# Experts of a PEER layer in batches of one pair in place of two, with the turns between the dense steps spread twice as finely

## The chip, the cores and the metric

The kernel runs on one core of a Trainium2 chip. The metric is the device time of one execution in microseconds (us).

## The reference

The program is a decoder trunk of two layers for 256 tokens of width 1024, all in fp32. A layer is a mixer (attention in three forms, a convolution and a pooling branch), a cross-attention, and a block of single-neuron experts. The change touches the last of these:

```python
s_half = einsum('thpc,pnc->thpn', q, sub_keys)          # 8 heads, 2 halves, 128 keys
v_half, i_half = top_k(s_half, 16)
... top_s, expert_idx = top 16 of the 256 sums, per head
gate = softmax(top_s)
act = gelu(einsum('cd,chkd->chk', hc, u[ic]))           # u row of each chosen expert, times the token
out = einsum('chk,chkd->cd', gate * act, v[ic])         # v rows, weighted and summed
```

Each token chooses 8 x 16 = 128 experts of 16384. A chosen expert costs one row of u and one of v, 1024 numbers each, which lie side by side in memory.

## The kernel before

**Tiles and stages.** The tokens form two tiles of 128, one token to a partition. With two layers there are four pairs of layer and tile. The program has five stages, and a stage runs the dense part of one (layer, tile) beside the experts of the one before it: a first stage (dense alone), a second (dense, experts, and the keys and values of the memory for layer 1), two turns of a loop that share one code, and a last stage (experts alone, then the final norm). The dense part is written out as a plan of some sixty steps (`mix_norm`, `zq`, `ab`, ..., `wo0`, `wo1`, `xa_norm`, ..., `ffn_norm`, `pq0`, ..., `rank0`), in the order in which every engine takes its share of them.

**A pair.** One of the 128 (head, k) choices is called a pair here; it means one expert for each of the 128 tokens. For pair k:

- POOL (`gather`, L424) multiplies a stacked identity by the pair's gate into `diag` (L426), and issues an indirect DMA that brings 128 rows of u and v, 8 KB each, into one slot of `uv_rows` (L429). There are `ROWS` = 10 slots. For pairs from 10 on it waits for the semaphore `slots_free`, that is, for PE to be through with the pair that held the slot. At a stage's end the first ten pairs of the next are issued the same way.
- DVE (L461) takes the product of the u rows and the tokens in `h_ps`, with the sum into `act_b`.
- ACT (`batch_run`, below) takes the gelu and scales `diag` by it (L908).
- PE (L1154) adds `diag` times the v rows into `acc_pe`, in four matmuls, and signals `slots_free`.

**Batches and turns.** DVE, ACT and PE are in-order engines. Each has a function `batch_run(b0, b1)` that does its share of the batches b0 to b1, with B = 2 pairs to a batch. The function `run` walks through the plan; behind each step it does the number of batches that a table names. The function `spread` makes that table: each step has a weight in `LENGTH`, and the batches done by the end of a step are `within` times the share of weight passed, rounded down. PE's table is `LAG` batches behind that of DVE and ACT. What is left over at the end is done behind the last step. ACT's share of the batches reads:

```python
for b in range(b0, b1):
    act.wait_ge(sems["dots_done"], b * B + B)
    s.activation(gelu_b[:, b % AHEAD, :], act_b[:, b % AHEAD, :], ACT.Gelu_apprx_tanh).then_inc(sems["gelu_done"], 1)
    act.wait_ge(sems["gelu_done"], b + 1)
    for k in range(b * B, b * B + B):
        ...
        s.activation(diag[:, slot_of(k), :], diag[:, slot_of(k), :], ACT.Copy,
                     scale=gelu_b[:, b % AHEAD, k % B:k % B + 1]).then_inc(sems["diag_done"], 1)
```

PE waits for `diag_done` of each pair, and DVE for the landing of each pair. Gelu, exp and sqrt need different tables in ACT, and a load stands where the function changes; Copy needs none of its own.

**Other transfers.** The weights of the dense products come as blocks of 2 MB into a ring of two (`w_ring`); SP issues the next one when PE has finished with the one before last. They share the 16 DMA engines with the pairs.

Of the kernel before, what the change touches and what calls it, by code (L numbers as in the profile page):

```python
# [37 lines left out]
THETA, ROT = 500000.0, HD // 4  # L38
HALF = ROT // 2

B = 2
NB = PAIRS // B
QUARTER = NB // 4
AHEAD = 5
ROWS = AHEAD * B
HT = P // 2
BLK = 512
# [19 lines left out]
for _name, _w in (("causal", S), ("cadd", NC), ("cvalid", NC), ("cur", 4 * P), ("prev", 4 * P), ("flag", 1)):  # L67
# [64 lines left out]
LAST_PLAN = ["rank1", "rank_pairs1", "gates1", "look_up1", "rank2", "rank_pairs2", "gates2", "look_up2", "rank3",  # L132
             "rank_pairs3", "gates3", "look_up3"]
# [5 lines left out]
          "sel_turn": 4, "win_scores": 7, "sel_out": 8, "conv_norm": 4, "win_turn": 4, "conv_act": 3, "conv_silu": 2,  # L139
          "win_out": 8, "small_branches": 3, "mix_turn": 2, "wo": 9, "xa_norm": 7, "xq": 8, "xa_scores": 6,  # L140
          "xa_turn": 4, "xa_out": 4, "xo": 9, "ffn_norm": 8, "pq": 8, "sub_scores": 2, "mem_kv": 8}
LAG = 1


def spread(plan, within):

    lengths = [LENGTH[name if name in LENGTH else name.rstrip("0123456789")] for name in plan]
    vector, tensor, done, passed = {}, {}, 0, 0
    for name, length in zip(plan, lengths):
        passed += length  # L150
        due = within * passed // sum(lengths)
        vector[name] = due - done
        tensor[name] = max(due - LAG, 0) - max(done - LAG, 0)
        done = due
    return {"vector": vector, "scalar": vector, "tensor": tensor}


TURNS = spread(PLAN, NB - 2)
MEM_TURNS = spread(MEM_PLAN, NB - 2)
LAST_TURNS = spread(LAST_PLAN, 20)  # L160


TURN_PARTS = [6.25]
# [26 lines left out]
def build_program(nc, a):  # L190
    with ExitStack() as ctx:
        def sb(name, shape, dt=F32):
            return ctx.enter_context(nc.sbuf_tensor(name, shape, dt))
# [46 lines left out]
        gate = sb("gate", [P, PAIRS])  # L240
        act_b = sb("act_b", [P, AHEAD, B])
        gelu_b = sb("gelu_b", [P, AHEAD, B])
        half_i = sb("half_i", [P, 16, TOPK], U32)
# [44 lines left out]
        def stage(dense, experts, mem_layer=None, first=False, last=False):  # L288


            plan = LAST_PLAN if last else FIRST_PLAN if first else PLAN if mem_layer is None else MEM_PLAN
            turns = {} if first else LAST_TURNS if last else TURNS if mem_layer is None else MEM_TURNS
            jobs = [job for name in plan for job in STEP_JOBS.get(name, ())]
# [19 lines left out]
            def slot_of(k):  # L313
                return k % ROWS

            def landed_by(k):

                uses = len(range(k % ROWS, PAIRS, ROWS))
                return (experts * uses + k // ROWS) * 16 + 16
# [50 lines left out]
            with nc.Block(no_gpsimd_drain=not last) as block:  # L370
# [82 lines left out]
                def _(dve):  # L453
# [3 lines left out]
                    def batch_run(b0, b1):  # L457
                        for k in range(b0 * B, b1 * B):
                            dve.wait_ge(landed[slot_of(k)], landed_by(k))
                            u_row = uv_rows[:, slot_of(k), 0, :]  # L460
                            v.tensor_tensor_reduce(u_row, u_row, h_ps[:, :], 1.0, 0.0, ALU.mult, ALU.add,  # L461
                                                   act_b[:, k // B % AHEAD, k % B:k % B + 1]).then_inc(
                                                       sems["dots_done"], 1)
# [431 lines left out]
                def _(act):  # L895
# [3 lines left out]
                    def batch_run(b0, b1):  # L899
                        for b in range(b0, b1):  # L900
                            act.wait_ge(sems["dots_done"], b * B + B)
                            s.activation(gelu_b[:, b % AHEAD, :], act_b[:, b % AHEAD, :],  # L902
                                         ACT.Gelu_apprx_tanh).then_inc(sems["gelu_done"], 1)
                            act.wait_ge(sems["gelu_done"], b + 1)
                            for k in range(b * B, b * B + B):
                                if k >= ROWS:
                                    act.wait_ge(sems["gates_spread"], k - ROWS + 1)
                                s.activation(diag[:, slot_of(k), :], diag[:, slot_of(k), :], ACT.Copy,  # L908
                                             scale=gelu_b[:, b % AHEAD, k % B:k % B + 1]).then_inc(
                                                 sems["diag_done"], 1)  # L910
# [672 lines left out]
```

## Time and profile before

| | |
|---|---|
| median of 3 runs | 1901.41 us (1895.86, 1901.41, 1905.76) |
| the profiled execution, its own time | 1897.98 us |
| its span | 1896.2 us |
| what lies around the span | 1.8 us |
| TensorE clock granted, mean | 0.852 of full |
| PE, DVE, ACT, POOL busy | 1375.9, 1133.7, 514.9, 677.6 us |
| DMA | 702.57 MB, mean 371 GB/s |

The busy times are sums over stages with different limits, so none of them says what bounds the kernel. The share of the DMA engines is read by stretch of time, and where it falls below 1 the timeline shows which engine held the next transfer back. A window row gives the stretch and its length, the busy time of PE, of PE's weight loads, of DVE, ACT and POOL (with the count of instructions in brackets), then the granted clock, the DMA share and GB/s.

### The profile page before, as it was taken

The page shows a single profiled execution, that of the slowest core. Times are in us where ns is not written, and L with a number is a line of the kernel's source. Part 1 is how long each engine was busy: PE and PEld are TensorE (multiplying, and loading weights), DVE is VectorE, ACT ScalarE, POOL GpSimd, SP SyncE. Part 2 cuts the span into 40 slices and gives each one's busy share as a digit, 9 for nine tenths or more (in the row PEclk, how much of TensorE's full clock was granted, in tenths as well). Part 3 has the DMA queues.
Part 4 walks back from the last instruction along what each step waited for, and adds up shares of the span by engine and source line. Part 5 has one row for each costly group of instructions (what it writes and reads, how often), then busy time and mean ns, then how long its engine had stood idle before and what let it go on. Part 6 is the DMA issues. An engine that isn't in the chain of part 4 may idle for free. (4 is left out here: it accounts for less than half of the span.)

```text
span 1896.2 us, 23075 instructions
## 1 busy us (share of the span) xinstructions
PE 1375.9 (73%) x8428; PEld 714.3 (38%) x8428; DVE 1133.7 (60%) x2788; ACT 514.9 (27%) x1311; POOL 677.6 (36%) x1028
## 2 busy tenths in 40 slices
PE   6899956767889983946878863957878874555554
PEld 4666752234554551412444631422444631111110
DVE  5431359876342477689743567688743579864444
ACT  3331122154221222223522222223522221211111
POOL 0000025433333352534433351434433354555551
PEclk9899978889899996977989895977989887777776
DMA  7434589998999999999999998999999999999996
GB/s 272 178 151 178 199 355 399 423 422 353 364 364 399 371 422 409 371 422 403 421 415 397 395 420 346 379 422 400 421 413 397 390 421 371 404 423 421 421 421 268
DMA packets 87380, 702.57 MB, mean 371 GB/s; under 512 B 9952, under 2 KB 10080, under 8 KB 12128
## 3 DMA queue, kind: packets, MB, share of 16 engines
q0 software_dynamic: 73728, 536.90, 68.9%
q1 hardware_dynamic: 13536, 164.15, 21.9%
q8 instruction: 69, 1.13, 0.2%
q14 instruction: 47, 0.39, 0.1%
HBM read 698.92 MB, written 2.10 MB: 370 GB/s over the span
## 5 line engine op out<-in xcount | busy, mean ns | idle before, releaser
L1154 PE MATMUL acc_pe<-uv_rows,diag 64*64 64x512 f32 x4096 | 622.1, 741 | 346.4 <-ACT diag L908 338.0
L461 DVE CUSTOM_DVE_ANT_0 uv_rows<-uv_rows,h_ps 128x1024 f32<-128x1024 f32 x512 | 603.0, 1218 | 196.4 <-DMA uv_rows<-uv_in,idx 191.5
L426 POOL TENSOR_TENSOR diag<-ident_st,gate 128x64 f32<-128x64 f32 x512 | 167.4, 327 | 1097.5 <-PE acc_pe L1154 832.9
L429 POOL DMA_INDIRECT uv_rows<-uv_in,idx x512 | 510.1, 996 | 84.3 <-issue 51.2
L1154 PEld LDWEIGHTS acc_pe<-uv_rows,diag 64*64 64x64 f32 x4096 | 160.3, 158 | 726.6 <-ACT diag L908 501.1
L902 ACT ACTIVATE gelu_b<-act_b 128x2 f32<-128x2 f32 x256 | 51.9, 203 | 901.5 <-DVE act_b L461 891.1
L1181 PE MATMUL bank<-h_t,w_ring 128*128 128x128 f32 x1792 | 210.5, 279 | 11.3 <-DMA w_ring<-blocks_in 9.1
L1181 PEld LDWEIGHTS bank<-h_t,w_ring 128*128 128x128 f32 x1792 | 205.8, 195 | 31.8 <-issue 29.0
L1181 PE MATMUL bank<-w_ring,h_t 128*128 128x512 f32 x448 | 201.0, 603 | 3.0 <-ACTq L944 3.0
L908 ACT ACTIVATE diag<-diag,gelu_b 128x64 f32<-128x64 f32 x512 | 150.2, 340 | 8.4
L1181 PEld LDWEIGHTS bank<-w_ring,h_t 128*128 128x128 f32 x448 | 84.2, 193 | 119.5 <-issue 115.6
L748 DVE TENSOR_TENSOR xs<-xs,bank 128x512 f32<-128x512 f32 (+1 forms) x16 | 11.0, 688 | 179.0 <-PE bank L1181 179.0
L1176 PE MATMUL bank<-ident,area 128*128 128x128 f32 x304 | 51.3, 324 | 87.1 <-ACT area L921 67.3
L941 ACT ACTIVATE area<-bank 128x512 f32<-128x512 f32 x96 | 56.2, 586 | 207.5 <-PE bank L1181 195.8
L1176 PEld LDWEIGHTS bank<-ident,area 128*128 128x128 f32 x304 | 41.5, 167 | 112.8 <-ACT area L921 69.6
L585 DVE SCALAR_TENSOR_TENSOR conv<-hc,smalls,conv 128x128 f32<-128x128 f32 x240 | 67.4, 355 | 0.1
L902 ACT ACT_TABLE_LOAD x45 | 57.7, 1283 | 1.6
L760 DVE TENSOR_REDUCE st<-bank 128x2 f32<-128x512 f32 x8 | 5.5, 692 | 68.5 <-PE bank L1181 68.5
L461 DVE DVE_READ_ACCUMULATOR2_ANT act_b<- 128x1 f32 x512 | 42.3, 83 | 0.0
L1432 PE MATMUL acc_pe<-xs,zero 128*128 128x512 f32 x16 | 14.9, 1085 | 30.3 <-issue 17.1
L782 DVE MAX8 half_v<-area 128x8 f32<-128x128 f32 x64 | 13.9, 279 | 38.1 <-ACTq L944 38.0
L1016 ACT ACTIVATE area<-area,st 128x256 f32<-128x256 f32 x64 | 31.9, 499 | 12.4 <-DVE st L654 11.1
(200 smaller groups left out, 1173.9 us busy)
## 6 DMA issues: line engine op xcount, KB each, us to landing
w_ring<-blocks_in SPq DMA_DIRECT2D x72, 2048.0 KB
uv_rows<-uv_in,idx POOLq DMA_INDIRECT x512
tcon<-tile_consts_in SPq DMA_DIRECT2D x4, 656.5 KB, 13.0
smalls<-smalls_in SPq DMA_DIRECT2D x3, 816.5 KB, 8.5
h_ffn<-ffn_gain_in SPq DMA_DIRECT2D x4, 512.0 KB
xs<-x_in SPq DMA_DIRECT2D x2, 512.0 KB, 10.6
uv_rows<-mem_in SPq DMA_DIRECT2D x1, 1024.0 KB, 16.3
mem_gained<-uv_rows SPq DMA_DIRECT2D x1, 1024.0 KB, 4.8
```

The lines of the kernel that those rows point to most:

```text
L426: nc.gpsimd.tensor_tensor(diag[:, slot_of(k), :], ident_st[:, :], gate[:, k:k + 1].to_broadcast([P, HT]), ALU.mult).then_inc(sems["gates_s ...
L429: nc.gpsimd.indirect_dma_start(uv_rows[:, slot_of(k), :, :].rearrange("p a n -> p (a n)"), None, a["uv"], bass.IndirectOffsetOnAxis(ap=idx ...
L461: v.tensor_tensor_reduce(u_row, u_row, h_ps[:, :], 1.0, 0.0, ALU.mult, ALU.add, act_b[:, k // B % AHEAD, k % B:k % B + 1]).then_inc(sems[" ...
L585: ins = v.scalar_tensor_tensor(out=conv[:, g, :], in0=hc[:, g, k:k + P], scalar=small("cw", g * CONV_W + k, 1), in1=conv[:, g, :], op0=ALU ...
L902: s.activation(gelu_b[:, b % AHEAD, :], act_b[:, b % AHEAD, :], ACT.Gelu_apprx_tanh).then_inc(sems["gelu_done"], 1)
L908: s.activation(diag[:, slot_of(k), :], diag[:, slot_of(k), :], ACT.Copy, scale=gelu_b[:, b % AHEAD, k % B:k % B + 1]).then_inc(sems["diag_ ...
L941: drain(s.activation(out, src, func, **kw), job)
L1016: s.activation(probs[:, h, :], probs[:, h, :], ACT.Exp, bias=st[:, 8 + h:9 + h], accum_out=st[:, col + h:col + h + 1]).then_inc(sems[done], 1)
L1154: mm = pe.matmul(acc_pe[c * HT:(c + 1) * HT, r * BLK:(r + 1) * BLK], diag[tok, slot_of(k), :], uv_rows[tok, slot_of(k), 1, c * BLK:(c + 1) ...
L1176: mm = pe.transpose(out[:, i * P:(i + 1) * P], src, ident[:, :])
L1181: mm = pe.matmul(out, lhs, rhs, start=(i == 0), stop=(i == len(pairs) - 1))
L1432: pe.matmul(acc_pe[:, c * 512:(c + 1) * 512], zero[:, :], xs[:, 0:512], start=True, stop=False, skip_group_check=True)
```

## The change

Three tables and constants change, and no function body:

```diff
-B = 2
+B = 1
 NB = PAIRS // B
 QUARTER = NB // 4
-AHEAD = 5
+AHEAD = 10
 ROWS = AHEAD * B
...
-LAG = 1
+LAG = 2
...
-TURNS = spread(PLAN, NB - 2)
-MEM_TURNS = spread(MEM_PLAN, NB - 2)
-LAST_TURNS = spread(LAST_PLAN, 20)
+TURNS = spread(PLAN, NB - 4)
+MEM_TURNS = spread(MEM_PLAN, NB - 4)
+LAST_TURNS = spread(LAST_PLAN, 40)
```

A batch is one pair, so ACT takes a gelu of one column for each pair, 128 for each stage with experts in place of 64. The slots stay 10, the lag of PE stays two pairs, and the pairs left over at the end stay four. The tables of turns are rounded down to one pair in place of two: behind a step, as many pairs are done as before or one more. 

On PE, at the start of the loop's stage, stand the products with `zero` that clear `acc_pe`, the pairs (four matmuls each), the transposes of `mix_norm` into `bank`, and the products of `zq` (`bank<-w_ring,h_t`) and `ab` (`bank<-h_t,w_ring`). Before:

```order
L1432 MATMUL acc_pe<-xs,zero 128x512 x2
L1154 MATMUL acc_pe<-uv_rows,diag 64x512 x24
L1176 MATMUL bank<-ident,area 128x128 x8
L1154 MATMUL acc_pe<-uv_rows,diag 64x512 x8
L1181 MATMUL bank<-w_ring,h_t 128x512 x8
L1154 MATMUL acc_pe<-uv_rows,diag 64x512 x16
```

and now:

```order
L1432 MATMUL acc_pe<-xs,zero 128x512 x2
L1154 MATMUL acc_pe<-uv_rows,diag 64x512 x28
L1176 MATMUL bank<-ident,area 128x128 x8
L1154 MATMUL acc_pe<-uv_rows,diag 64x512 x8
L1181 MATMUL bank<-w_ring,h_t 128x512 x8
L1154 MATMUL acc_pe<-uv_rows,diag 64x512 x12
```

Seven pairs in place of six stand ahead of the transposes, nine in place of eight ahead of `zq`, and twelve in both ahead of `ab`.

On ACT, at the start of the second stage, stand the square sum of the norm (L917), its root (L919) and the scaling (L921), and the pairs. Before:

```order
L894 UNCONDITIONAL_BRANCH
L917 ACTIVATE h_t,st<-xs 128x1024
L919 ACT_TABLE_LOAD
L919 ACTIVATE st<-st 128x1
L921 ACTIVATE area<-xs,st 128x1024
L902 ACT_TABLE_LOAD
L902 ACTIVATE gelu_b<-act_b 128x2
L908 ACTIVATE diag<-diag,gelu_b 128x64 x2
```

and now:

```order
L894 UNCONDITIONAL_BRANCH
L902 ACT_TABLE_LOAD
L902 ACTIVATE gelu_b<-act_b 128x1
L908 ACTIVATE diag<-diag,gelu_b 128x64
L917 ACTIVATE h_t,st<-xs 128x1024
L919 ACT_TABLE_LOAD
L919 ACTIVATE st<-st 128x1
L921 ACTIVATE area<-xs,st 128x1024
```

The first pair, which waits for DVE's `rank1` and its own dot product, stands ahead of the norm.

On ACT, in the loop's stage, the exp of the compressed scores (L1021) is followed by the eight exps of the selected scores (L1016). Before:

```order
L1021 ACT_TABLE_LOAD
L1021 ACTIVATE p_cmp<-p_cmp 128x128
L1016 ACTIVATE area,st<-area,st 128x256 x8
L902 ACT_TABLE_LOAD
L902 ACTIVATE gelu_b<-act_b 128x2
L908 ACTIVATE diag<-diag,gelu_b 128x64 x2
```

and now:

```order
L1021 ACT_TABLE_LOAD
L1021 ACTIVATE p_cmp<-p_cmp 128x128
L902 ACT_TABLE_LOAD
L902 ACTIVATE gelu_b<-act_b 128x1
L908 ACTIVATE diag<-diag,gelu_b 128x64
L1016 ACT_TABLE_LOAD
L1016 ACTIVATE area,st<-area,st 128x256 x8
L902 ACT_TABLE_LOAD
```

One pair now parts the two groups of exps, with a table load ahead of it and one behind it. Over the program ACT gets 7 more table loads: 3 in the second stage and 2 in each turn of the loop.

## Rows read from the trace of the kernel before

**Rows 1.** The page: GB/s in 40 slices of the span.

```profile
GB/s 272 178 151 178 199 355 399 423 422 353 364 364 399 371 422 409 371 422 403 421 415 397 395 420 346 379 422 400 421 413 397 390 421 371 404 423 421 421 421 268
```

**Rows 2.** Windows: the second stage, the loop's two turns, the last stage.

```profile
258.00:714.00 456.00, 359.54 (x2183) 194.31 (x2184) 277.43 (x684) 130.52 (x328) 169.91 (x257) 0.89 0.97 393
714.00:1139.00 425.00, 302.17 (x1991) 154.31 (x1991) 278.66 (x684) 125.67 (x320) 170.96 (x256) 0.86 0.99 406
1139.00:1561.00 422.00, 310.87 (x1992) 157.89 (x1992) 279.11 (x685) 126.08 (x321) 170.16 (x256) 0.84 0.97 399
1561.00:1896.00 335.00, 183.36 (x1028) 44.90 (x1028) 209.42 (x465) 62.62 (x208) 153.65 (x236) 0.72 0.95 391
```

**Rows 3.** Timeline, DVE, last stage: two dot products, 20 pairs apart (start, length, ..., idle before).

```profile
1728.76 1.22 DVE L461 CUSTOM_DVE_ANT_0 uv_rows<-uv_rows,h_ps 128x1024 f32<-128x1024 f32 x1 [1.25 <-DMA uv_rows<-uv_in,idx]
...
1778.48 1.22 DVE L461 CUSTOM_DVE_ANT_0 uv_rows<-uv_rows,h_ps 128x1024 f32<-128x1024 f32 x1 [1.26 <-DMA uv_rows<-uv_in,idx]
```

**Rows 4.** Windows of single holes in the DMA share.

```profile
450.00:468.00 18.00, 14.41 (x97) 8.38 (x90) 6.36 (x14) 5.24 (x14) 7.90 (x12) 0.93 0.71 250
...
754.00:770.00 16.00, 14.88 (x64) 6.38 (x68) 14.26 (x32) 4.60 (x14) 3.82 (x6) 0.82 0.68 240
...
1174.00:1196.00 22.00, 15.69 (x68) 6.69 (x72) 15.99 (x40) 8.95 (x21) 3.91 (x7) 0.71 0.48 168
...
1574.00:1590.00 16.00, 7.70 (x52) 2.26 (x48) 13.16 (x29) 5.17 (x12) 9.91 (x14) 0.71 0.88 315
```

**Rows 5.** Timeline, the loop's second turn, around its `mix_norm`.

```profile
1172.27 1.22 DVE L461 CUSTOM_DVE_ANT_0 uv_rows<-uv_rows,h_ps 128x1024 f32<-128x1024 f32 x1
...
1173.42 1.22 DVE L461 CUSTOM_DVE_ANT_0 uv_rows<-uv_rows,h_ps 128x1024 f32<-128x1024 f32 x1
...
1182.28 3.69 PE L1154 MATMUL acc_pe<-uv_rows,diag 64*64 64x512 f32 x16 [0.83 <-DVE h_t L493]
...
1184.37 0.29 POOL L426 TENSOR_TENSOR diag<-ident_st,gate 128x64 f32<-128x64 f32 x1 [14.57 <-PE acc_pe L1154]
```

**Rows 6.** Timeline, the start of the last stage.

```profile
1567.37 1.22 DVE L461 CUSTOM_DVE_ANT_0 uv_rows<-uv_rows,h_ps 128x1024 f32<-128x1024 f32 x1
...
1574.21 0.29 POOL L426 TENSOR_TENSOR diag<-ident_st,gate 128x64 f32<-128x64 f32 x1 [0.29 <-PE acc_pe L1154]
...
1580.07 0.29 POOL L426 TENSOR_TENSOR diag<-ident_st,gate 128x64 f32<-128x64 f32 x1 [4.44 <-PE acc_pe L1154]
```

**Rows 7.** Timeline, the end of the last pair.

```profile
1878.71 1.22 DVE L461 CUSTOM_DVE_ANT_0 uv_rows<-uv_rows,h_ps 128x1024 f32<-128x1024 f32 x1 [1.22 <-DMA uv_rows<-uv_in,idx]
...
1880.61 3.69 PE L1154 MATMUL acc_pe<-uv_rows,diag 64*64 64x512 f32 x16 [3.22 <-ACT diag L908]
```

**Rows 8.** Timeline, the start of the second stage.

```profile
264.87 0.15 DVE L485 TENSOR_SCALAR st<-st 128x1 f32<-128x1 f32 x1
...
274.98 9.11 PE L1181 MATMUL bank<-h_t,w_ring 128*128 128x128 f32 x64 [6.31 <-DMA w_ring<-blocks_in]
...
285.22 0.29 POOL L426 TENSOR_TENSOR diag<-ident_st,gate 128x64 f32<-128x64 f32 x1 [27.01 <-PE acc_pe L1154]
```

**Rows 9.** Timeline, the loop's first turn, between `cmp_scores` and `sel_turn`.

```profile
886.37 0.51 ACT L1016 ACTIVATE area<-area,st 128x256 f32<-128x256 f32 x1
...
893.37 3.43 PE L1154 MATMUL acc_pe<-uv_rows,diag 64*64 64x512 f32 x16 [5.94 <-ACT diag L908]
...
902.48 0.20 DVE L660 RECIPROCAL st<-st 128x8 f32<-128x8 f32 x1
```

**Rows 10.** Timeline, PE ahead of the second stage's `wo0`.

```profile
463.91 1.95 PE L1154 MATMUL acc_pe<-uv_rows,diag 64*64 64x512 f32 x16 [2.01 <-ACT diag L908]
```

**Rows 11.** The page's groups: the gelu, the scaled `diag`, the table loads.

```profile
L902 ACT ACTIVATE gelu_b<-act_b 128x2 f32<-128x2 f32 x256 | 51.9, 203 | 901.5 <-DVE act_b L461 891.1
...
L908 ACT ACTIVATE diag<-diag,gelu_b 128x64 f32<-128x64 f32 x512 | 150.2, 340 | 8.4
L902 ACT ACT_TABLE_LOAD x45 | 57.7, 1283 | 1.6
```

## Prediction

> **What bounds the kernel now.** I began with the slices of GB/s [rows 1]. The first five slices move 151 to 272 GB/s, and from the sixth on the rate sits near 421 wherever it is not interrupted. No engine comes near its span. So from the second stage on the transfers are the limit, with holes. The windows by stage [rows 2] give the holes: against 422 GB/s, the second stage (456 us at 393) lacks 31 us of transfer, the loop's turns (425 at 406, 422 at 399) lack 16 and 23, and the last stage (335 at 391) lacks 25, of which 20 are the end, behind the last landing. In steady state a pair lands every (1778.48 - 1728.76) / 20 = 2.49 us [rows 3], which is the price of one pair in transfer time.
>
> A hole opens when all ten slots are waited for: ten pairs give 24.9 us of cover. I looked at who ends the wait. The largest hole, 1174 to 1196 [rows 4], lies in the loop's second turn: 22 us at 168 GB/s are 13.2 us without transfer. Its rows [rows 5] show DVE's dot products of a batch at 1172.27 and 1173.42; the norm follows on ACT, and PE takes that batch only behind the norm's transposes, at 1182.28. POOL had waited 14.57 us. The same place in the first turn (754 to 770) is a hole of 6.9 us, the one at 450 to 468 is 7.3 us, and the last stage has one of 4.1 us at 1574 to 1590 [rows 4]. So what the change is worth is read from when slots come free beside the dense steps.
>
> **The change, part by part.**
>
> *The gelu for each pair.* A first pair of a batch no longer waits for its neighbour's dot product. Two dots start 1173.42 - 1172.27 = 1.15 us apart [rows 5] (1.14 below), so the first of two slots comes free 1.14 us sooner where PE waits for it; the second comes when it did. The price is 256 more gelus of 203 ns [rows 11], 52 us of ACT over the 1638 us of rows 2, in which ACT is busy 445 us. For one pair ACT needs 0.20 + 0.34 and a gap, some 0.6 us, against 1.14 of DVE, so this is hidden under DVE; without that cover it would be 0.2 us a pair.
>
> *The table of turns.* Behind a step, 0 or 1 more pair is done. One more pair released ahead of a hole puts 2.49 us of transfer into it; its dot delays the dense chain behind it by 1.14 us, less the 0.25 by which the last diag of a batch is sooner. At the hole of rows 5, seven pairs stand ahead of the transposes in place of six, and nine in place of eight ahead of `zq`: gain 2.5 - 0.9 = 1.6 us. The end of the stage before adds something: PE's last two pairs were one batch, now only one is left behind the last dot, 0.98 us at the upper clock (1.95 for two [rows 10]). Sum 2.6 us for each turn, **5.2 us** for both. Behind this hole come stretches where DVE waits for transfers, so it is not given back.
>
> *Later holes of the loop.* Those at `wo0` and `ffn_norm` are small (the rest of the 16 and 23 us, in pieces of 1 to 4). PE is the chain there and by `pq0` one pair more has been done ahead of the norm, at a delay of about 0.9 us. I take 1 us for each turn, **2 us**; the bounds are 0 (the chain alone counts) and 2.49.
>
> *The second stage.* At its start the first pair moves ahead of the norm on ACT [rows 8]. The square sum lay under DVE's `rank1`, whose end shows as DVE's norm step at 264.87. Now it waits for `rank1` and a dot (1.22), the gelu and diag (0.6) and its own length (about 1.2): the norm step comes at 267.9 in place of 264.87, and then the root's table load (1.28), which lay under `rank1`, stands open. The norm is 4.4 us later. PE does not mind: `ab` waited 6.31 us for its weights until 274.98. The first slot now comes free at about 275 and not at 285.22, and that closes the 1.2 us hole of 282 to 286. DVE, which paces this stretch, loses 3.2 us and is one pair (1.14) ahead. I count +2 -1.2, about +1. Ahead of `wo0` PE waited 2.01 us for a fresh batch [rows 10]; only one fresh pair is needed now and the second need not be awaited: -2. Two norms (`xa_norm`, `ffn_norm`) are later by 1.05 and 0.8, and one pair more is done when the last hole of the stretch ends: -2.5. Sum about **-1.6 us**; bounds +4.4 (the whole delay of the norm on the chain, nothing won) and -7.
>
> *The last stage.* At its start the first slot needs one dot, not two, and three pairs in place of two are done ahead of `rank_pairs1`. The two gathers at 1574.21 and before are followed by none until 1580.07 [rows 6]; the third falls into this hole of 4.1 us: **-2.5 us**. What else the last stage lacks of its 25 us (25 - 20 - 4.1, about 1) I take as filled: **-1**; the bound is 0. At the end the last pair lands and its dot starts at 1878.71; PE then runs two pairs in 3.69 us [rows 7]; one remains: **-1.8 us**.
>
> *The table loads.* There are 7 more of 1283 ns [rows 11], 9.0 us on ACT. Those in the loop part the exps: the first exp at 886.37 [rows 9] moves by 1.28 + 0.54 + 1.28 = 3.1 us. PE then waits longer than its 5.94 us at 893.37, but DVE is busy without a pause through this stretch and needs the exps next at 902.48 [rows 9]; so I price the loads at nothing, with DVE as cover. Without the cover they cost 9.0, and the upper bound takes them.
>
> ScalarE: Activation LUTs in the Trainium skill ("What ACT_TABLE_LOAD costs") puts a switch at about 2.66 us, a load of 1283 ns and as much again for draining. The load's figure is the trace's own. With the drain the seven loads would come to 18.6 us; nothing in the rows here shows the drain as a time of its own.
>
> *Sum.* 5.2 + 2 + 1.6 + 2.5 + 1 + 1.8 = 14.1 us. Against the profiled execution (span 1896.2 plus 1.8 around it, 1897.98) this is 1884; that execution lies 3.4 us below the median of the runs shown, so on the scale of the median 1901.4 - 14.1 = **1887**.
>
> **Rivals.**
>
> - *Nothing but the end (no change).* The holes come back elsewhere: within a stretch where PE or DVE is the chain, one pair moved ahead leaves one fewer in the next turn (12 in both programs ahead of `ab`), and the hole behind is larger by what the one before lost. For it: in the second stage from 450 to 655 the holes come one after another. Against it: DVE waits for landings again behind both `mix_norm` holes and through the whole last stage, which keeps what was won. It leaves the tail and the start of the last stage, 1.8 + 2.5 = 4.3 of gain, and gives some of it back to the norm delays: 1898.
> - *ACT's share becomes the chain (slower).* Each norm that has one more pair ahead of it is later by about 1 us (2 in the second stage, 2 in each turn), the second stage's first norm by 4.4, and the parted exps push each turn by 3.1: 6 + 4.4 + 6.2 = 16.6, and only the tail (1.8) is won: 1916. It decides if slots wait for ACT in the stretch of rows 9, which takes a delay that eats up the time between PE's pairs at 893.37 and DVE's need at 902.48, 9 us. Against it: in that stretch the rate is at 421, with a backlog of several pairs.
> - *The clock.* In the last stage PE gets two pairs every 4.97 us, at a mean granted clock of 0.72 [rows 2]; it moves between 1.2 and 2.4 GHz. Now it gets one every 2.49. If the clock stayed at 1.2 GHz, a pair would take 1.85 us (3.69 for two), still under 2.49. The last stage would not feel it; a lower clock in the second stage's long products would, and 1% more PE time of 360 us is 3.6 us: 1891.
>
> **How the numbers follow.** The forecast (transfer holes partly filled, 1876 to 1892) gets 0.55; no change but the end, 0.28; slower through ACT, 0.12; the clock, 0.05. A measurement of this kernel can tell 0.5%, 9.5 us, from no change. Under 1892 lies most of the first case: faster 0.54. Slower than 1911 is most of the ACT case: 0.11. The rest, 0.35, is within. The range takes in the filling of every hole of one pair's size once (about 12 of 2.49 us, 30 us: 1872) and, on the other side, table loads uncovered (9.0) with nothing won but the tail, 1908. So 1872 to 1908.
>
> **What would show it.** Right: POOL's wait at the loop's `mix_norm` stays but one more gather lies ahead of it; GB/s in the slices with 346, 371 and 353 rises; the last PE group behind the last dot is 1.8 us long; the time of DVE at L461 is unchanged. Wrong: PE's waits for `diag` grow in sum outside the last stage; the second stage is longer than 456 us; `ab` starts later than 17 us into the second stage; the hole at 1174 is as long as before. If the second stage's start costs more than 3 us, or DVE turns out to wait for the parted exps, the prediction is too low.

## The result and the profile after

The changed kernel takes **1887.5 us** (median of 5 runs, 1883.99 to 1889.42) against 1900.24 us for the kernel before on the same chip (5 runs): a ratio of **0.9934**, 95% interval [0.9913, 0.9956]. That is 12.7 us less; the forecast was 14.1 less. The profiled execution took 1888.95 us (span 1887.2), 9.0 us less than that of before.

The page of the changed kernel: busy time of the engines, GB/s in 40 slices, and the groups that answer to [rows 11] (with PE's products for the pairs, which waited 338.0 us for `diag` before).

```profile
PE 1425.4 (76%) x8428; PEld 715.2 (38%) x8428; DVE 1133.2 (60%) x2788; ACT 595.8 (32%) x1574; POOL 675.3 (36%) x1028
...
GB/s 268 179 156 179 188 349 391 416 422 333 357 381 380 387 420 419 366 423 389 421 422 405 396 421 420 326 422 393 422 422 414 404 420 419 393 421 421 421 421 289
...
L1154 PE MATMUL acc_pe<-uv_rows,diag 64*64 64x512 f32 x4096 | 655.4, 754 | 306.1 <-ACT diag L908 293.2
...
L908 ACT ACTIVATE diag<-diag,gelu_b 128x64 f32<-128x64 f32 x512 | 178.1, 348 | 17.0 <-ACT gelu_b L902 0.2
...
L902 ACT ACTIVATE gelu_b<-act_b 128x1 f32<-128x1 f32 x512 | 102.5, 200 | 808.9 <-DVE act_b L461 788.1
L902 ACT ACT_TABLE_LOAD x49 | 62.9, 1283 | 9.2 <-issue 7.8
```

ACT does what was announced: 512 gelus of 200 ns, and over all its lines 111 table loads in place of 104. Nobody's total tells why the time fell; that is read by stage. The windows of the changed kernel for the stages of [rows 2], each from its own start:

```profile
259.00:718.50 459.50, 369.21 (x2184) 196.21 (x2184) 277.70 (x684) 151.37 (x395) 167.28 (x256) 0.86 0.96 390
718.50:1141.00 422.50, 315.31 (x1991) 158.19 (x1991) 278.17 (x684) 145.80 (x386) 171.48 (x256) 0.83 0.99 407
1141.00:1556.00 415.00, 315.34 (x1991) 158.43 (x1991) 278.74 (x684) 145.76 (x386) 171.25 (x256) 0.83 0.98 404
1556.00:1887.00 331.00, 205.59 (x1028) 39.39 (x1028) 209.43 (x465) 82.84 (x272) 152.11 (x236) 0.68 0.96 398
```

The second stage became longer, all the others shorter. The start of a stage is DVE's copy into `h_ps` in the timeline. Its lengths in us, for the kernels that the argument needs (one profiled execution each; the first stage, which has no pairs, differs by up to 3 us from one to the other, and so does this much of any sum). A profiled execution need not be a typical one: that of `e1` took 1884.83 us, its median is 1878.75. The loop is the same code in the changed kernel, `e3` and `e4`, and one of its turns differs by up to 5.8 us among them, so a smaller difference of one turn says little. The second stage repeats better (`e4`, `e8` and `e12` share it: 452.1, 452.1 and 453.1):

| | second | loop 1 | loop 2 | last |
|---|---|---|---|---|
| before | 455.8 | 425.2 | 421.5 | 335.4 |
| after | 459.6 | 422.7 | 415.0 | 331.1 |
| e1_old_tables | 455.0 | 419.8 | 415.2 | 331.7 |
| e2_old_tables_wait_two | 459.6 | 428.2 | 423.9 | 335.5 |
| e3_second_stage_old_table | 454.0 | 418.3 | 417.9 | 331.5 |
| e4_norm_first | 452.1 | 420.4 | 412.1 | 332.0 |
| e11_nine_slots | 466.7 | 427.6 | 426.4 | 333.5 |

Where the transfers stood still in a stretch is its length times (422 - GB/s) / 422, as in the prediction. Windows of the kernel before: the first 60 us of each turn of the loop (`mix_norm`), 100 us late in each turn (`wo0` to `ffn_norm`), and the first 100 us of the last stage.

```profile
714.00:774.00 60.00, 31.62 (x151) 12.97 (x152) 50.10 (x158) 14.71 (x36) 16.16 (x24) 0.70 0.92 372
...
974.00:1074.00 100.00, 84.21 (x549) 52.64 (x550) 41.72 (x96) 26.39 (x64) 33.19 (x52) 0.90 0.97 393
1139.00:1199.00 60.00, 32.26 (x143) 12.53 (x144) 50.12 (x158) 14.54 (x35) 15.39 (x23) 0.63 0.82 328
...
1399.00:1499.00 100.00, 82.56 (x534) 50.97 (x535) 40.15 (x87) 28.03 (x66) 34.15 (x53) 0.90 0.97 389
1561.00:1661.00 100.00, 53.49 (x292) 14.64 (x292) 90.26 (x269) 23.45 (x65) 48.03 (x71) 0.70 0.98 390
```

The same stretches of the changed kernel:

```profile
719.00:779.00 60.00, 33.14 (x147) 12.31 (x146) 50.53 (x160) 17.94 (x48) 16.36 (x24) 0.65 0.93 378
...
979.00:1079.00 100.00, 86.87 (x563) 53.74 (x564) 43.55 (x99) 29.87 (x78) 34.47 (x54) 0.88 0.99 401
1141.00:1201.00 60.00, 34.20 (x139) 12.18 (x140) 50.62 (x159) 17.64 (x46) 15.52 (x23) 0.64 0.86 345
...
1401.00:1501.00 100.00, 88.12 (x574) 55.56 (x575) 44.71 (x100) 29.43 (x78) 34.47 (x54) 0.87 1.00 408
1556.00:1656.00 100.00, 54.05 (x292) 14.18 (x292) 90.80 (x270) 29.36 (x83) 47.75 (x72) 0.70 1.00 406
```

Idle transfer time at `mix_norm` fell from 7.1 to 6.3 and from 13.4 to 10.9 us, late in the turns from 6.9 to 5.0 and from 7.8 to 3.3, at the start of the last stage from 7.6 to 3.8. So the late holes gave more than the large one. `e3` and `e4`, with the same loop, show how far such sums scatter: 15.2 and 14.3 us for both turns at `mix_norm` (20.5 before, 17.2 in the changed kernel), 4.3 and 2.6 late (14.7 and 8.3).

At the end ([rows 7]) one pair is left behind the last dot product. Timeline of the changed kernel:

```profile
1871.75 1.83 PE L1154 MATMUL acc_pe<-uv_rows,diag 64*64 64x512 f32 x8 [0.49 <-ACT diag L908]
1872.30 1.22 DVE L461 CUSTOM_DVE_ANT_0 uv_rows<-uv_rows,h_ps 128x1024 f32<-128x1024 f32 x1 [1.22 <-DMA uv_rows<-uv_in,idx]
...
1874.19 1.09 PE L1154 MATMUL acc_pe<-uv_rows,diag 64*64 64x512 f32 x8 [0.61 <-ACT diag L908]
```

From the start of the last dot to the end of PE's last product it was 1884.30 - 1878.71 = 5.59 us and is 1875.28 - 1872.30 = 2.98: 2.6 us won, where 1.8 was forecast. The pair before took 1.83 us and the last 1.09, so the clock rose to its upper level just there (granted 0.52 from 1869.0 to 1873.5, 1.00 from 1873.5 to 1876.0). That 0.7 us is luck: at the lower level the end would have won 1.9, the forecast's 1.8, and the last pair of `e1` took 1.99 us.

### The profile page after: what moved, and what is told of

Read it like the earlier page. It is cut to its first block and busy times, and to the rows that moved or that the text cites. A ratio compares the mean times of both kernels' runs of the same rounds, so it can differ in the third digit from the quotient of the medians.

```text
span 1887.2 us, 23579 instructions
## 1 busy us (share of the span) xinstructions
PE 1425.4 (76%) x8428; PEld 715.2 (38%) x8428; DVE 1133.2 (60%) x2788; ACT 595.8 (32%) x1574; POOL 675.3 (36%) x1028
## 5 line engine op out<-in xcount | busy, mean ns | idle before, releaser
L1154 PE MATMUL acc_pe<-uv_rows,diag 64*64 64x512 f32 x4096 | 655.4, 754 | 306.1 <-ACT diag L908 293.2
L1154 PEld LDWEIGHTS acc_pe<-uv_rows,diag 64*64 64x64 f32 x4096 | 145.8, 156 | 719.3 <-ACT diag L908 568.6
L902 ACT ACTIVATE gelu_b<-act_b 128x1 f32<-128x1 f32 x512 | 102.5, 200 | 808.9 <-DVE act_b L461 788.1
L908 ACT ACTIVATE diag<-diag,gelu_b 128x64 f32<-128x64 f32 x512 | 178.1, 348 | 17.0 <-ACT gelu_b L902 0.2
L1176 PE MATMUL bank<-ident,area 128*128 128x128 f32 x304 | 55.6, 345 | 79.4 <-ACT area L921 66.9
L1176 PEld LDWEIGHTS bank<-ident,area 128*128 128x128 f32 x304 | 45.4, 178 | 106.1 <-ACT area L921 68.2
L1432 PE MATMUL acc_pe<-xs,zero 128*128 128x512 f32 x16 | 14.6, 1065 | 31.0 <-issue 16.5
L1016 ACT ACTIVATE area<-area,st 128x256 f32<-128x256 f32 x64 | 31.8, 498 | 11.5 <-DVE st L654 11.3
## 6 DMA issues: line engine op xcount, KB each, us to landing
xs<-x_in SPq DMA_DIRECT2D x2, 512.0 KB, 10.9
```

The lines of the kernel that those rows point to most:

```text
L1016: s.activation(probs[:, h, :], probs[:, h, :], ACT.Exp, bias=st[:, 8 + h:9 + h], accum_out=st[:, col + h:col + h + 1]).then_inc(sems[done], 1)
L1154: mm = pe.matmul(acc_pe[c * HT:(c + 1) * HT, r * BLK:(r + 1) * BLK], diag[tok, slot_of(k), :], uv_rows[tok, slot_of(k), 1, c * BLK:(c + 1) ...
L1176: mm = pe.transpose(out[:, i * P:(i + 1) * P], src, ident[:, :])
L1432: pe.matmul(acc_pe[:, c * 512:(c + 1) * 512], zero[:, :], xs[:, 0:512], start=True, stop=False, skip_group_check=True)
```

## The experiments

Ratios are against the kernel before, timed in turn with it on the same chip. Batches are of one pair except in `e2` and `e5`, as told.

### The wait or the table (e1, e2)

`e1_old_tables`: gelu, diag and PE go by single pairs, but the tables are those of before, counted in twos.

```diff
-TURNS = spread(PLAN, NB - 4)
+TURNS = spread_by_two(PLAN, PAIRS // 2 - 2)
...
+        due = within * passed // sum(lengths)
+        vector[name] = 2 * (due - done)
+        tensor[name] = 2 * (max(due - 1, 0) - max(done - 1, 0))
```

(and so for the other two tables). 

> The changed kernel with the tables of turns of the kernel before (each turn counted in pairs, so the same pairs stand behind the same steps); only the gelu for each pair is left of the change. Baseline 1900.2 us before, 1887.5 us changed. Theory A (most of the gain is slots that come free earlier because a pair no longer waits for its neighbour): about 1890. Theory B (the gain is from the finer tables, one more pair ahead of a hole): about 1898, only the end of each stage (1 to 2 us) is won. Theory C (the second stage, 3.8 us longer in the trace of the changed kernel, lost by its table): the second stage is back at 456 us, so if A is right too the time falls below 1887.

`e2_old_tables_wait_two`: the same, and ACT waits again for the dots of both pairs before the first gelu. It has the wait of before, the order of before, and 256 more gelus.

```diff
-act.wait_ge(sems["dots_done"], b * B + B)
+act.wait_ge(sems["dots_done"], b // 2 * 2 + 2)
```

> The kernel with the old tables, one gelu for each pair, but ACT waits for the dot products of both pairs of two before it takes the first of the two gelus, as before. So it has the price of 256 more gelus (52 us of ACT) and none of the earlier release. If the gelus are hidden: 1900 within 3 us. If they cost where PE waits for diag: up to 0.2 us for each of the waits, 1905 to 1910. The difference to the run with the old tables and no such wait is the worth of the earlier release alone: theory A 8 to 10 us, theory B 2 to 4 us.

Measured: `e1` 1878.75 us, **0.9901** [0.9882, 0.992]; `e2` 1902.83 us, **1.0029** [1.0015, 1.0042] (the kernel before on this chip: 1897.14). The wait alone is worth 24.1 us, nearly twice what the whole change brought; the largest expectation, theory A, had 8 to 10. The 256 gelus, with the wait behind each and the `diag` scalings that now take 348 ns in place of 340, cost 0.3%, 5.5 us (2.8 to 8.0). The finer tables bring nothing on top: the changed kernel lies 0.3% above `e1` (the intervals just overlap).

The start of the last stage shows the wait alone. Timeline of `e2`, then of `e1` (a line is 13 further down in these kernels; L479 is the start of the stage):

```profile
1570.05 1.23 DVE L479 COPY h_ps<-h_ffn 128x1024 f32<-128x1024 f32 x1 [2.92 <-PEq L1479]
...
1579.30 0.35 ACT L921 ACTIVATE diag<-diag,gelu_b 128x64 f32<-128x64 f32 x1
...
1581.80 0.29 POOL L439 TENSOR_TENSOR diag<-ident_st,gate 128x64 f32<-128x64 f32 x1 [11.97 <-PE acc_pe L1167]
```

```profile
1551.34 1.23 DVE L479 COPY h_ps<-h_ffn 128x1024 f32<-128x1024 f32 x1 [2.40 <-PEq L1479]
...
1559.44 0.35 ACT L921 ACTIVATE diag<-diag,gelu_b 128x64 f32<-128x64 f32 x1
...
1561.94 0.29 POOL L439 TENSOR_TENSOR diag<-ident_st,gate 128x64 f32<-128x64 f32 x1 [10.82 <-PE acc_pe L1167]
```

The first `diag` comes 9.25 us behind the start of the stage in `e2` and 8.10 in `e1`, and POOL's wait for a slot is 11.97 and 10.82 us: 1.15 us both times, one dot product. Where the pairs come one by one as they land, the neighbour is further away. The steady part of the last stage in `e2`, then in `e1`:

```profile
1781.99 0.08 DVE L474 DVE_READ_ACCUMULATOR2_ANT act_b<- 128x1 f32 x1
...
1784.59 0.20 ACT L915 ACTIVATE gelu_b<-act_b 128x1 f32<-128x1 f32 x1 [3.91 <-DVE act_b L474]
```

```profile
1781.50 0.08 DVE L474 DVE_READ_ACCUMULATOR2_ANT act_b<- 128x1 f32 x1
1781.61 0.20 ACT L915 ACTIVATE gelu_b<-act_b 128x1 f32<-128x1 f32 x1 [1.90 <-DVE act_b L474]
```

The gelu of a first pair starts 2.60 us behind its dot product in `e2` and 0.11 in `e1`: the wait is 2.49 us, the time from one landing to the next, and not the 1.14 of a dot product. How the 24.1 us divide between places of the one kind and of the other was not measured.

The same stretches as above, in `e2` and then in `e1`, show where transfer time was won (late in the first turn, `mix_norm` of the second, late in the second, start of the last stage):

```profile
978.00:1078.00 100.00, 82.75 (x525) 50.49 (x522) 38.80 (x78) 30.68 (x78) 33.52 (x54) 0.88 0.97 389
1146.00:1206.00 60.00, 31.98 (x141) 12.29 (x142) 49.81 (x157) 16.05 (x42) 15.19 (x22) 0.63 0.83 332
...
1406.00:1506.00 100.00, 83.69 (x533) 51.83 (x534) 39.94 (x85) 29.36 (x76) 33.66 (x53) 0.88 0.97 389
1570.00:1670.00 100.00, 54.72 (x292) 14.93 (x292) 89.55 (x268) 27.37 (x83) 46.98 (x70) 0.70 0.97 386
```

```profile
976.00:1076.00 100.00, 88.10 (x584) 56.25 (x588) 45.54 (x103) 29.05 (x79) 33.43 (x53) 0.89 1.00 409
1136.00:1196.00 60.00, 33.29 (x148) 13.11 (x149) 50.06 (x158) 17.85 (x47) 15.35 (x24) 0.64 0.86 343
...
1396.00:1496.00 100.00, 88.37 (x584) 56.39 (x588) 45.44 (x103) 29.16 (x80) 33.51 (x54) 0.89 1.00 410
1551.00:1651.00 100.00, 53.22 (x292) 14.00 (x292) 90.60 (x270) 29.37 (x83) 48.12 (x73) 0.74 0.99 400
```

Late in the turns the idle time falls from 7.8 to 3.1 and from 7.8 to 2.8 us, at the second turn's `mix_norm` from 12.8 to 11.2 (at the first turn's, 352 and 374 GB/s, from 10.0 to 6.8), in the last stage from 8.5 to 5.2.

### The second stage (e3, e4)

`e3_second_stage_old_table` is the changed kernel with the old table in the second stage alone. `e4_norm_first` keeps the new tables and only moves the first pair of the second stage back behind the norm, on DVE and ACT.

```diff
-MEM_TURNS = spread(MEM_PLAN, NB - 4)
+MEM_TURNS = spread_by_two(MEM_PLAN, PAIRS // 2 - 2)      # e3
...
+MEM_TURNS["vector"]["mix_norm"] += MEM_TURNS["vector"]["rank1"]      # e4
+MEM_TURNS["vector"]["rank1"] = 0
+MEM_TURNS["scalar"] = MEM_TURNS["vector"]
```

> The changed kernel, with only the second stage back on the table of turns of before. The trace of the changed kernel has this stage 3.8 us longer. If its table is the reason: the stage takes 455 to 456 us or less and the time is about 1883.5. Rival: the stage is longer because the gelus for each pair or a lower TensorE clock hold up PE there, then it stays near 459 us and the time at 1887.

> The changed kernel, where the second stage's first pair is done behind the first norm and no longer behind rank1, on DVE and ACT; all else as changed. Theory: the norm of the second stage, 2.9 us later in the trace of the changed kernel, is back, and this delay is the greater part of the 3.8 us: about 1884.5. Rival: the delay is absorbed (the product ab waits for its weights) and the loss comes from later turns of that stage: 1887, and the stage still takes about 459 us.

Measured: `e3` 1880.06 us, 0.9898 [0.9878, 0.9918]; `e4` 1880.33 us, 0.9911 [0.989, 0.9932]. The four kernels `e1`, `e3`, `e4` and the changed one overlap in part; the stages tell more. `e4` has the shortest second stage of the table, 452.1 us against 459.6. The start of the second stage in the changed kernel ([rows 8] is that of before):

```profile
266.82 0.20 ACT L902 ACTIVATE gelu_b<-act_b 128x1 f32<-128x1 f32 x1 [6.34 <-DVE act_b L461]
...
268.48 0.15 DVE L485 TENSOR_SCALAR st<-st 128x1 f32<-128x1 f32 x1 [1.69 <-ACT h_t L917]
...
270.19 1.15 ACT L921 ACTIVATE area<-xs,st 128x1024 f32<-128x1024 f32 x1 [0.23 <-DVE st L488]
...
276.10 8.92 PE L1181 MATMUL bank<-h_t,w_ring 128*128 128x128 f32 x64
```

and in `e4` (lines 4 further down):

```profile
260.31 1.06 ACT L921 ACTIVATE h_t<-xs 128x1024 f32<-128x1024 f32 x1 [7.66 <-PEq L1470]
...
266.66 0.15 DVE L489 TENSOR_SCALAR st<-st 128x1 f32<-128x1 f32 x1
...
267.28 1.15 ACT L925 ACTIVATE area<-xs,st 128x1024 f32<-128x1024 f32 x1 [0.23 <-DVE st L492]
```

The stage starts at 258.95 and at 260.06. In the changed kernel ACT stands 6.34 us in front of the gelu before it takes the square sum, and DVE's norm step comes 9.53 us behind the start; in `e4` the square sum is done long ahead and the step comes at 6.60. So one pair ahead of the norm costs 2.9 us there, and 4.0 at the scaling (11.24 and 7.22 behind the start), where the root's table load comes in. The difference grows on the way: 5.0 us at the step behind `xo1`, 7.5 at the stage's end. The windows show two stretches in which the changed kernel's transfers stand still longer than before: 60 to 80 us into the stage (388 GB/s before, 329 in the changed kernel, 387 in `e4`) and 160 to 180 us (421, 369 and 384). The first, 2.8 us, is gone with the norm in front; the second, 2.5 us, stays for the most part (1.8 in `e4`). What opens them was not followed engine by engine.

### Table loads (e8)

`e8_scores_together` is `e4`, and in the loop the pair that parted the exps is moved behind the second group; 106 table loads are left of 110.

```diff
+TURNS["vector"]["sel_scores"] += TURNS["vector"]["cmp_scores"]
+TURNS["vector"]["cmp_scores"] = 0
+TURNS["scalar"] = TURNS["vector"]
```

> The changed kernel with the second stage's norm ahead of its first pair (1880.3 us, 0.991), and also, in the loop, the pair that parts the exp of the compressed scores from those of the selected scores moved behind the latter, on DVE and ACT. That takes two of the seven added table loads out of each of the loop's two turns (2 x 1.28 us and the 0.54 of the pair, ahead of eight exps). If the loads are hidden under DVE, as the prediction has it: no change, within 1.5 us of 1880.3. If ACT is the chain there: 3 us less in each turn, about 1874.

Measured: 1882.02 us, 0.9908 [0.9886, 0.9929], against 0.9911 of `e4`: no difference. The loads in the loop are hidden, as far as this can tell: the other case, some 6 us or 0.3% less, lies at the edge of the two intervals. What one costs while it shows, in the changed kernel, at the place where one pair now parts the exps:

```profile
891.10 1.28 ACT L1021 ACT_TABLE_LOAD   x1
892.41 0.31 ACT L1021 ACTIVATE p_cmp<-p_cmp 128x128 f32<-128x128 f32 x1
892.73 1.28 ACT L902 ACT_TABLE_LOAD   x1
894.03 0.20 ACT L902 ACTIVATE gelu_b<-act_b 128x1 f32<-128x1 f32 x1
```

The exp starts 1.31 us behind the start of its load and the gelu 1.30: the load's 1.28 and nothing more. ScalarE: Activation LUTs in the Trainium skill ("What ACT_TABLE_LOAD costs") has about 2.66 us for a switch, half of it a drain; in these rows there is no room for it.

### How far PE lags (e5, e6, e7, e9, e10)

All shift PE's table against that of DVE and ACT. `e5_two_lag_four` is the kernel before, with batches of two and `LAG = 2`, four pairs; `e6_one_lag_one`, `e10_old_tables_lag_three` and `e7_one_lag_four` are `e1` with one, three and four pairs; `e9_norm_first_lag_three` is `e4` with three.

```diff
-LAG = 1
+LAG = 2      # e5
...
-        tensor[name] = 2 * (max(due - 1, 0) - max(done - 1, 0))
+        tensor[name] = max(2 * due - 1, 0) - max(2 * done - 1, 0)      # e6; with 3 in e10, with 4 in e7
...
-LAG = 2
+LAG = 3      # e9
```

> The kernel before (batches of two), with PE four pairs behind DVE and ACT in the table in place of two. The old tables with one pair to a batch gave a ratio of 0.990, and with the wait for both dot products put back 1.003, so the wait for the neighbour is worth 1.3%. Two mechanisms could carry it. Theory S (slots: the first of two slots comes free 1.14 us sooner, and holes in the transfers shrink): here slots come free later, so the time rises above 1900, to 1910 or more. Theory C (chain: PE stands in front of a dense step waiting for a fresh diag, and everything behind is later): with four pairs of lag the diags are no longer fresh, so this kernel wins most of the 18 to 24 us without any change of the batch, 1880 to 1890.

> One pair to a batch, old tables, PE one pair behind in place of two (1878.8 us with two). Theory S: slots come free a step sooner, so 1872 to 1877. Theory C: PE waits ahead of its dense steps for a diag that is one pair fresher, so it loses some of what the batch of one gave: 1885 to 1895.

> One pair to a batch, old tables, PE four pairs behind in place of two (1878.8 us with two). Theory S: slots later, above 1885. Theory C: no fresh diags at all, 1879 or a little less, as the waits that are left go. If both act, the two effects cancel near 1880 to 1885.

> The new tables with the first norm of the second stage ahead of the first pair, and PE's table three pairs behind DVE's and ACT's in place of two. Two forces set the best lag. A slot comes free later by what lies between the pair's dot and PE's turn; a shorter lag, on the other hand, lets PE wait for diags that ACT makes in the same turn. Measured so far with batches of one pair: lag one 1.069, two 0.990, four 1.008. If a turn of three pairs makes PE wait for a fresh diag at lag two (the new tables have turns of three, with one fresh pair each), lag three takes that wait away and wins: below 0.990, PE's waits for diag under 270 us. If late slots weigh more already at this point, the time lies between lag two and lag four, about 0.998, and the idle time of the transfers grows from 74 to some 88 us.

> Batches of one pair, the tables of the kernel before counted in pairs of two, PE three pairs behind. With turns of two and four pairs, lag two has no fresh pair in a turn of two and two in a turn of four; lag three one in a turn of four. If late slots weigh more: about 0.998, halfway between 0.990 (lag two) and 1.008 (lag four). If the fresh pairs of the turns of four cost as much as the slots: about 0.990.

| pairs of lag | 1 | 2 | 3 | 4 |
|---|---|---|---|---|
| batches of two, old tables | | 1 (before) | | 1.0142 [1.0118, 1.0166] |
| of one, old tables | 1.0688 [1.066, 1.0715] | 0.9901 | 0.9939 [0.9926, 0.9952] | 1.0082 [1.006, 1.0104] |
| of one, new tables, norm first | | 0.9911 | 0.9927 [0.9913, 0.9941] | |

With a longer lag PE's waits for `diag` do fall (with the old tables 270.6 us at two pairs, 266.5 at three, 233.5 at four) and the time rises, because a slot comes free later: in `e9` the first 60 us of the first turn run at 363 GB/s in place of the 398 of `e4`, 8.4 us idle in place of 3.4, and its late holes, now gone (422 GB/s in 100 us, against 410), don't make up for it. `e7` against `e1` is 1.8%, `e5` against the kernel before 1.4%. So theory S holds for a longer lag: time goes with the slots, not with PE's waits. The idea that the turns of three in the new tables would do better at lag three falls: 0.9927 against 0.9911 is no gain. Both lags of three came out between the two values that had been expected.

With a lag of one pair PE's waits for `diag` rise from the 270.6 us of `e1` to 421.2, and POOL's for slots to 972.7 (820.1 in `e1`). At 1.0688, 2026.44 us, `e6` is far beyond both expectations (1872 to 1877, and 1885 to 1895): theory C has the direction, but a loss of 6 to 16 us where it is some 150. The timeline of `e6` at one of the products for the memory (`bank<-area,w_ring` into `mem_k`), and behind one of DVE's rank steps:

```profile
604.79 1.09 PE L1167 MATMUL acc_pe<-uv_rows,diag 64*64 64x512 f32 x8
...
604.90 0.60 ACT L954 ACTIVATE mem_k<-bank 128x512 f32<-128x512 f32 x1 [7.81 <-PE bank L1194]
...
606.25 2.81 PE L1167 MATMUL acc_pe<-uv_rows,diag 64*64 64x512 f32 x24 [0.37 <-ACT diag L921]
...
814.89 1.99 PE L1167 MATMUL acc_pe<-uv_rows,diag 64*64 64x512 f32 x8 [6.88 <-ACT diag L921]
```

ACT takes the bank first, then the pairs of its turn; PE has one pair ready and then waits for them, here for 0.37 us. The long waits lie elsewhere: at 814.89 PE had stood 6.88 us for a pair whose dot product DVE takes behind its rank step. Up to the last stage PE stops for `diag` 133 times in `e6`, 45 of them for more than 2 us, and 64 and 26 times in `e1`. How these waits add up to 8% was not worked out.

### Slots, and one more pair ahead (e11, e12)

`e11_nine_slots` is `e4` with nine slots in place of ten. `e12_one_more_ahead` is `e4`, and in the loop one pair is moved from behind `zq` to ahead of `mix_norm`, on DVE, ACT and PE. That is the prediction's rule for a hole, by itself.

```diff
-AHEAD = 10
+AHEAD = 9      # e11
...
+for _engine in ("vector", "tensor"):      # e12
+    TURNS[_engine]["rank2"] += 1
+    TURNS[_engine]["zq"] -= 1
```

> The new tables with the norm first, and nine slots for pairs in place of ten (rows of act_b and gelu_b too). If a hole opens when all slots are waited for, nine slots give 22.4 us of cover in place of 24.9, and each hole that is there now grows by up to 2.49 us; there are four or five in the second stage and three or four in each of the loop's turns, some 11 in all: up to 27 us, and new small ones beside them; 1.000 to 1.008, with the idle time of the transfers at 95 to 110 us in place of 74. If the holes were set by the chain of the dense steps alone, the time stays at 0.991.

> The kernel with the norm first in the second stage (ratio 0.991), and in the loop's table one more pair behind the step ahead of mix_norm on DVE, ACT and PE, and one fewer behind zq. This is the prediction's rule for a hole, alone: the pair puts 2.49 us of transfer into the hole and its dot delays the norm and PE's next pairs by 1.14 less 0.25, so 1.6 us for each turn, 3.2 us in all: ratio 0.989 to 0.990, and what the first 60 us of a turn lack of 422 GB/s falls from 10.9 us (second turn) to some 9.3. The rival: DVE's chain is what ends the hole, so the delay eats the pair (0.991, 10.9 us as before, and POOL's long wait starts a pair later and ends later), or costs more than it brings (0.992 or more) because the pair moved ahead is missing behind zq.

Measured: `e11` 1915.02 us, 1.008 [1.0067, 1.0093], 1.7% or 32 us above `e4` by the ratios, the upper edge of what was expected: the second stage is 14.6 us longer, the turns 7.2 and 14.3, the last 1.5. So the holes do depend on the number of slots; the chain of the dense steps alone does not set them. `e12` 1880.23 us, 0.9899 [0.9883, 0.9916]: 0.1% under `e4`, within the intervals. Windows of `e4` and of `e12` for the second turn, its first 60 us and the late 100:

```profile
1133.00:1193.00 60.00, 34.68 (x146) 12.78 (x147) 50.54 (x160) 17.92 (x48) 16.17 (x24) 0.65 0.86 345
...
1393.00:1493.00 100.00, 88.52 (x612) 54.80 (x612) 49.45 (x110) 30.57 (x85) 36.86 (x58) 0.93 1.01 423
```

```profile
1131.00:1191.00 60.00, 34.95 (x142) 12.20 (x143) 50.61 (x159) 17.75 (x46) 16.34 (x24) 0.64 0.90 361
...
1391.00:1491.00 100.00, 86.20 (x584) 54.23 (x584) 45.84 (x103) 31.59 (x82) 34.40 (x54) 0.91 1.00 413
```

At `mix_norm` the idle time falls from 10.9 to 8.7 us, by 2.2, where the rule gives 1.6; late in the same turn it comes back, from nothing to 2.1. In the first turn the pair brings nothing at `mix_norm` (3.4 and 3.7 us), where the hole is small. A pair moved ahead fills the hole it is moved to and leaves one fewer for the next, in this kernel with nothing left at the end that could be measured.

## Why the prediction was right, and where it was not

The total was right to 1.4 us: 12.7 measured, 14.1 forecast. It was right as a sum only, and that is luck: the worth of the earlier release, forecast much too small, is offset by what the tables were to win and did not, and by costs that were priced at nothing. The terms are these (idle transfer time in us, and stage lengths of the profiled executions):

| step | forecast | measured |
|---|---|---|
| hole at `mix_norm`, both turns | -5.2 | -3.3 (20.5 to 17.2) |
| later holes of the loop | -2 | -6.4 (14.7 to 8.3) |
| second stage | -1.6 | +3.8 |
| a hole where the exps are parted, both turns | not named | +2.9 (3.9 to 6.8) |
| last stage, start and rest | -3.5 | -3.8 |
| last stage, end | -1.8 | -2.6 |
| more gelus (`e2` against before) | 0 | +5.5, inside the others |
| more table loads | 0 | 0 (4 of the 7 taken away in `e8`) |

The terms of the changed kernel add up to -9.4 us; the profiled executions differ by 9.0. Each is read from one execution, and by the scatter of `e3` and `e4` those of the loop are good to some 3 to 6 us.

- **What the gain comes from.** The prediction gave most of it to the table ("one more pair released ahead of a hole"), and counted the release of a first pair, 1.14 us sooner, as something that matters "where PE waits for it". It is the other way round. With the old tables the release alone brings 24.1 us less the 5.5 that the gelus cost (`e1`, `e2`); the tables add nothing that can be measured (`e3` and `e4` lie with `e1`), and most of what the changed kernel loses against these is seen in the second stage. The step that failed is the sizing of the gelu for each pair: 1.14 us at a few places in the prediction, 24.1 us in all in `e1` against `e2`. The wait for the neighbour is 1.15 us where both pairs have landed and 2.49 where they come as they land, and PE takes fresh pairs at many places. That it works by slots held back, and not by PE being late itself, is what `e5`, `e7` and `e11` speak for.
- **Later holes.** Priced at 1 us a turn with 2.49 as the bound; they gave 3.2 a turn, and in `e1` against `e2` some 4.8. The bound was wrong too: it was for one pair once, while the stretch has several turns in which PE waits for a fresh pair. That these add up is the likely reason; the waits were not counted one by one.
- **A new hole.** 160 to 180 us into each turn, where one pair now parts the exps, the transfers fell from 390 and 371 GB/s to 346 and 354, and to 355 and 343 in `e3`, 332 and 351 in `e4` (`e1`, with the old tables: 381 and 386). So it comes with the finer table; but neither the table loads nor the pair between the exps makes it, for `e8`, which has taken both away, still has it (349 and 347). What makes it is open.
- **The hole at `mix_norm`.** Smaller than forecast in this execution, -3.3; with the same loop `e3` has -5.3 and `e4` -6.2, so the 5.2 is not refuted. Of it 2.5 is there with the old tables too (`e1`, 18.0 us). POOL's wait there did become shorter, 12.93 us in place of the 14.57 of [rows 5]. The rule of one more pair is true where it is put (2.2 us for 1.6 in `e12`), but is given back further on. The rival of no change named this, and for the table it holds: against `e1` the new tables win 0.8 to 3.7 us at `mix_norm` and lose 3.2 to 4.1 where the exps are parted.
- **The second stage.** Forecast 1.6 shorter, was 3.8 longer: near the upper bound of +4.4. The later norm was foreseen in place and size (4.4 us with the root's load, 4.3 by the prediction's own terms, and 4.0 measured), and at its start the slots came free as foreseen: POOL's first gather stands 17.33 us into the stage in place of 26.96, and the first 42 us run at 424 GB/s in place of 412. But in the 150 us behind that the idle time rose from 1.4 to 6.8 us, in the two stretches told above, and the gains that were to outweigh the delay (-2, -2.5) came to 0.8 (29.2 to 28.4 us idle in the rest of the stage). What failed is to count them as won behind a later chain, and to look for no hole between. The prediction named it as what would make it wrong: a second stage over 456 us (459.6), and `ab` later than 17 us into the stage (276.10 - 258.95 = 17.15). With the norm in front of the first pair (`e4`) the stage is 3.7 shorter than before.
- **The last stage.** Start and end as forecast, with luck in both. Before, the end lacked 17.1 us (1861 to 1896: 35 us at 216 GB/s) and not 20, so 7.6 us of hole stood at the start where the prediction saw 5.1; and 0.7 of the end is the clock. By its length (-4.4) the stage won less than both terms together: 331 us at 398 GB/s are more bytes than 335 at 391, worth 1.8 us of transfer, so more of the rows came inside this stage; why was not traced.
- **The gelus.** Priced at nothing under DVE; `e2` shows 0.3% for them and what goes with them. Of 52 us of ACT one tenth surfaces.
- **The table loads.** Those in the loop are hidden, as the prediction had it; that of the second stage's root stands open and is part of the 4.0 us.
- **The rivals.** PE's waits for `diag` fell, from 338.0 to 293.2 us, and without the last stage from 198.1 to 180.6, so ACT's share did not become the chain. The clock did fall (0.852 to 0.828 in the mean, 0.72 to 0.68 in the last stage), and PE's busy time rose by 49.5 us; between kernels this shows no price, for `e1`, at 0.825 to 0.838, is as fast as any. Within `e1` the execution at 0.825 is the slowest of six, 1884.83 us, and the others took 1877.97 to 1881.76 at 0.832 to 0.838; which of the two follows the other no run shows, so a price of a few us is not excluded.
- **The signs.** The slices of 346, 371 and 353 GB/s in [rows 1] were to rise; they stand at 326, 366 and 333. Slices shift against the stages and can't tell; the windows by stage do.

The kernels `e1`, `e3`, `e4`, `e8` and `e12` all lie at 0.990 to 0.991 of before, some 0.3% below the changed kernel, whose interval overlaps with each of theirs; among themselves the measurement does not tell them apart.

## What to carry to other kernels

When a batch is split, price first each place where the consumer waits for a fresh element: there the whole wait for the neighbour comes off the buffer's hold, and there may be many such places. Price the wait by what paces the neighbour: here 1.14 us when it is the dot product, 2.49 when it is the landing. A finer table of turns brought nothing by itself here; look at each step that it moves ahead of a norm or another head of a chain, and put the chain's head first. The lag between producer and consumer has a best value on both sides of which time is lost (here, with the old tables, two pairs: one is 8% slower, three 0.4%, four 1.8%), and one slot of ten is worth 1.7%.

## What the runs showed of the hardware that was not expected

- TensorE fed with one pair every 2.49 us in place of two every 4.97 gets a lower granted clock, 0.68 in the last stage for 0.72, with the same products. `e1` and `e2` differ in nothing but the wait and have 0.66 and 0.74 there. At the very end of the changed kernel it rose from one pair to the next, from 1.83 us a pair to 1.09. The last stage became 4.4 us shorter all the same; in the other stages no run separates its price.
- A switch of ACT's table costs the 1.28 us of the load and 0.02 to 0.03 beside it, in the rows above.
- A gelu of one column takes 200 ns and one of two 203 ns: the price is that of the instruction, and halving the batch doubles it.
